# Thirty-two experts in 16 rounds instead of 18: fixed experts share their rounds with three of the smallest

## The reference, cut to what matters

```python
g_logits = (xt @ lp['rg_w'] + lp['rg_b']).astype(jnp.float32)
_, g_idx = lax.top_k(g_logits, 1)                       # 1 of 4 groups
...
top_v, top_i = lax.top_k(e_logits, TOP_K)               # 2 of its 8 experts
expert_idx = g_idx * EXPERTS_PER_GROUP + top_i
...
def run(args):
    xb, e = args
    return (jax.nn.silu(xb @ wg[e]) * (xb @ wu[e])) @ wd[e]
...
return jnp.einsum('nk,nkd->nd', w, ys[slot])
```

## Time and profile before

| | |
|---|---|
| three runs | 1404.47, 1409.8, 1411.97 us, median 1409.8 |
| profiled execution | 1408.7 us, its span 1406.9 us |
| PE, DVE, ACT, POOL busy | 87%, 51%, 20%, 8% of the span |
| mean DMA rate | 238 GB/s over the span |
| `up` (L2160), U and ring tiles | 174.9 + 132.4 us busy |
| `down` (L2193), U and ring tiles | 90.8 + 50.7 us busy |
| gathers (L580), scatters (L587) | 36 and 36 |

### The profile page before, as it was taken

The page is one execution under the profiler, slowest core; times in us unless marked ns, Lnnn a source line. Parts: engine busy times, 40 slices in busy tenths (PEclk is TensorE's granted clock), DMA queues, the critical chain, the costliest instruction groups (busy, mean ns, idle before and its releaser), DMA issues.

```text
span 1406.9 us, 19405 instructions
## 1 busy us (share of the span) xinstructions
PE 1218.9 (87%) x7082; PEld 710.5 (50%) x7082; DVE 722.8 (51%) x1639; ACT 284.4 (20%) x708; POOL 112.9 (8%) x171
## 2 busy tenths in 40 slices
PE   5999999889886798999959999988989579898891
PEld 3455545554452565566424554556445356566560
DVE  3365877782476132332362687877643723332334
ACT  1211153750121000000022103357211110000000
POOL 2000000001001111111000000000100011111100
PEclk9999999999888999999989999999999779999996
DMA  9321101347149999999960201014562399999996
GB/s 375 150 94 50 54 17 61 129 177 308 41 177 401 416 418 418 418 418 417 410 252 31 90 33 60 1 68 181 198 252 104 138 398 418 417 418 417 419 415 250
DMA packets 61199, 334.54 MB, mean 238 GB/s; under 512 B 11856, under 2 KB 11856, under 8 KB 29100
## 3 DMA queue, kind: packets, MB, share of 16 engines
q1 hardware_dynamic: 45504, 295.78, 52.2%
q0 software_dynamic: 15600, 37.50, 7.0%
HBM read 322.41 MB, written 27.61 MB: 249 GB/s over the span
## 4 chain that ended last, share of the span: by engine, by line
PE 50%; DMA 27%; DVE 10%; issue 4%; ACT 3%; DVEq 2%; SPq 1%; PEld 1%; POOL 1%; PEldq 0%; ACTq 0%; POOLq 0%
DMA U<-in_stream 14%; PE bank L1748 12%; PE bank L1679 9%; PE bank L2160 8%; DMA ring<-in_stream 8%; PE bank L2193 6%; PE bank L2047 4%; DMA U<-in_n2row 3%; PE bank L1623 1%; DVE U L1267 1%; PE bank L1836 1%; DMA U<-moe_out 1%; PE bank L1862 1%; PE bank L2141 1%; SPq L382 1%
## 5 line engine op out<-in xcount | busy, mean ns | idle before, releaser
L2160 PE MATMUL bank<-U,HT 128*64 128x256 f32 (+2 forms) x1088 | 174.9, 400 | 24.2 <-DMA U<-in_stream 16.5
L1748 PE MATMUL bank<-HT,ring 128*128 128x512 f32 (+1 forms) x640 | 175.4, 435 | 2.0 <-issue 2.0
L1679 PE MATMUL bank<-ring,HT 128*128 128x512 f32 x320 | 147.0, 601 | 2.9 <-ACT HT L649 1.5
L2160 PEld LDWEIGHTS bank<-U,HT 128*64 128x64 f32 (+2 forms) x1088 | 117.8, 147 | 62.4 <-issue 40.1
L2160 PE MATMUL bank<-ring,HT 128*64 128x256 f32 (+2 forms) x736 | 132.4, 402 | 12.8 <-DMA ring<-in_stream 9.1
L1748 PEld LDWEIGHTS bank<-HT,ring 128*128 128x128 f32 x640 | 97.3, 191 | 79.7 <-issue 79.7
L1110 DVE SCALAR_TENSOR_TENSOR U<-U,prm 128x655 f32<-128x655 f32 x120 | 107.9, 899 | 8.0 <-issue 0.8
L2160 PEld LDWEIGHTS bank<-ring,HT 128*64 128x64 f32 (+2 forms) x736 | 86.4, 154 | 46.2 <-issue 28.6
L2047 PE MATMUL bank<-ring,HT 128*128 128x512 f32 x240 | 106.6, 594 | 0.0
L1541 DVE TENSOR_TENSOR HT<-bank,HT 128x256 f32<-128x256 f32 x36 | 15.3, 424 | 174.4 <-ACT HT L879 174.4
L2193 PE MATMUL bank<-U,HT 128*64 128x512 f32 (+2 forms) x288 | 90.8, 596 | 9.5 <-DMA U<-in_stream 6.0
(11 more groups left out here) (363 smaller groups left out, 1652.2 us busy)
## 6 DMA issues: line engine op xcount, KB each, us to landing
ring<-in_stream SPq DMA_DIRECT2D x138, 1024.0 KB, 7.3
U<-in_stream SPq DMA_DIRECT2D x96, 1024.0 KB, 22.7
RAB<-in_stream SPq DMA_DIRECT2D x16, 1024.0 KB
U<-moe_out SPq DMA_DIRECT2D x20, 512.0 KB, 7.4
U<-in_stream SPq DMA_DIRECT2D x16, 512.0 KB
CAT<-in_stream SPq DMA_DIRECT2D x16, 512.0 KB
RAB<-mod_rows POOLq DMA_DIRECT2D x12, 512.0 KB, 8.8
moe_in<-CAT POOLq DMA_DIRECT2D x10, 512.0 KB, 3.3
```

The source lines that it names most:

```text
L1679: ins = e.matmul(bank[:], HT[:, k, t * P:(t + 1) * P], wide(q, k), start=(k == 0), stop=(k == KD - 1))
L1748: ins = e.matmul(out, wt(q)[:, k, P * (n % 2):P * (n % 2) + P], HT[:, k, lo:lo + w], start=(k == 0), stop=(k == KD - 1))
L2160: ins = e.matmul(PS[2 + p][s, FF * j:FF * j + FF], xgT[:, p, k, s], w, start=(k == 0), stop=(k == KD - 1))
```

## The change

The three rounds F keep their fixed expert, but give it 96 slots instead of 128: 64 in one half of the block and 32 in the next quarter. The last 32 slots take one of the three smallest experts. So 29 others remain to be placed: 4 in B, 14 in P, 8 in Q and 3 beside the fixed ones. That makes 16 rounds, in the order P P F P F Q B P F B P B Q B P P. The third fixed expert moves from round 11 to round 8.

`sides(r)` now returns for an F round three pieces, of which the first two use the same tile. In odd blocks the halves are swapped. `whole` says whether a piece is the last one that reads its tile; only there the place is released. The loader still loads the fixed experts' nine tiles first, and the small experts' tiles of F rounds in the order of use.

```diff
-FIXED, BIGS, MIDS, SMALLS = 3, 8, 16, 8
+FIXED, BIGS, MIDS, SMALLS = 3, 7, 14, 8
 NR = BIGS + MIDS // 2 + SMALLS // 4
+BESIDE = BIGS + MIDS + SMALLS
-ROUNDS = list("PPFPFQBPBPPFBQBBPP")
+ROUNDS = list("PPFPFQBPFBPBQBPP")
 def round_blocks():
-    blocks = {"F": [(n, (n,)) for n in range(FIXED)],
+    blocks = {"F": [(n, (n, BESIDE + n)) for n in range(FIXED)],
...
 def tiles_loaded():
-    return sorted(tiles_used(), key=lambda tile: ROUNDS[tile[0]] != "F")
+    blocks = round_blocks()
+    return sorted(tiles_used(), key=lambda tile: blocks[tile[0]][1][tile[2]] >= FIXED)
...
+                apart, beside = small(1280, NE), small(1320, NE)
                 e.tensor_scalar(capm, rank, float(BIGS), float(HALF), ALU.is_lt, ALU.mult)
                 e.tensor_scalar(step, rank, float(BIGS + MIDS), float(QUART), ALU.is_lt, ALU.mult)
                 e.scalar_tensor_tensor(out=at0, in0=rank, scalar=float(BIGS + MIDS), in1=rank, op0=ALU.min, op1=ALU.add)
-                e.tensor_scalar(small(1660, NE), rank, float(BIGS), 2.0, ALU.min, ALU.mult); dr()
+                e.tensor_scalar(small(1660, NE), rank, float(BIGS), 2.0, ALU.min, ALU.mult)
+                e.tensor_scalar(apart, rank, float(FIXED), float(-QUART), ALU.is_lt, ALU.mult)
+                e.tensor_scalar(beside, rank, 3.0, float(3 - 4 * BESIDE - 3 * BIGS - MIDS), ALU.mult, ALU.add); dr()
                 e.tensor_tensor(capm, capm, step, ALU.add)
-                e.tensor_tensor(at0, at0, small(1660, NE), ALU.add); dr()
+                e.tensor_tensor(at0, at0, small(1660, NE), ALU.add)
+                e.scalar_tensor_tensor(out=beside, in0=rank, scalar=float(BESIDE), in1=beside, op0=ALU.is_ge, op1=ALU.mult); dr()
+                e.tensor_tensor(capm, capm, apart, ALU.add)
+                e.tensor_tensor(at0, at0, beside, ALU.add); dr()
                 e.tensor_scalar(at0, at0, float(QUART), None, ALU.mult)
...
                 def sides(r):
-                    n = P // len(blocks[r][1])
-                    return [(a, slice(n * a, n * a + n)) for a in range(P // n)]
+                    n, lanes_of = blocks[r]
+                    if n < FIXED:
+                        q = 64 * (n % 2)
+                        return [(0, slice(q, q + 64), False), (0, slice(64 - q, 96 - q), True), (1, slice(96 - q, P - q), True)]
+                    w = P // len(lanes_of)
+                    return [(a, slice(w * a, w * a + w), True) for a in range(P // w)]
...
-                        for a, s in both:
+                        for a, s, whole in both:
                             key = (l, r, j, a)
                             w = half_tile(key, k // 4)[:, FF * (k % 4):FF * (k % 4) + FF]
                             ins = e.matmul(PS[2 + p][s, FF * j:FF * j + FF], xgT[:, p, k, s], w,
                                            start=(k == 0), stop=(k == KD - 1))
...
-                            if k == KD - 1:
-                                if j and (a, s) == both[-1]:
+                            if k == KD - 1 and whole:
+                                if j and s == both[-1][1]:
```

More of the change, by code:

```diff
@@ L69, in round_blocks @@
 def round_blocks():
-    blocks = {"F": [(n, (n,)) for n in range(FIXED)],
-              "B": [(n, (n,)) for n in range(FIXED, BIGS)],
-              "P": [(BIGS + n, tuple(BIGS + 2 * n + (a + n) % 2 for a in range(2))) for n in range(MIDS // 2)],
-              "Q": [(BIGS + MIDS // 2 + n, tuple(BIGS + MIDS + 4 * n + (a + 2 * n) % 4 for a in range(4))) for n in range(SMALLS // 4)]}
+    blocks = {"F": [(n, (n, BESIDE + n)) for n in range(FIXED)],
+              "B": [(n, (n,)) for n in range(FIXED, BIGS)]}
+    for kind, first, lane, w in (("P", BIGS, BIGS, 2), ("Q", BIGS + MIDS // 2, BIGS + MIDS, 4)):
+        count = (MIDS if w == 2 else SMALLS) // w
+        blocks[kind] = [(n, tuple(lane + w * (n - first) + (a + n % 2 * w // 2) % w for a in range(w)))
+                        for n in range(first, first + count)]
     return [blocks[kind].pop(0) for kind in ROUNDS]
@@ L2161, in up @@
                                            start=(k == 0), stop=(k == KD - 1))
-                            if k == 0 and (a, s) == both[-1]:
+                            if k == 0 and s == both[-1][1]:
                                 settle(ins)
-                            if k == KD - 1:
-                                if j and (a, s) == both[-1]:
+                            if k == KD - 1 and whole:
+                                if j and s == both[-1][1]:
                                     ins.then_inc(S["gu_ps"], 1)
@@ L2194, in down @@
                                                start=(k == 0), stop=(k == 1))
-                                if k == 0 and j == 0 and (a, s) == both[-1]:
+                                if k == 0 and j == 0 and s == both[-1][1]:
                                     settle(ins)
-                                if k and j:
-                                    if (a, s) == both[-1]:
+                                if k and j and whole:
+                                    if s == both[-1][1]:
                                         ins.then_inc(S["y2_ps"], 1)
```

## The result

| | median us | runs | ratio to before, with its interval |
|---|---|---|---|
| before | 1410.88 | 1404.47 to 1412.26 | |
| after | 1433.2 | 1423.97 to 1435.01 | 1.0154 [1.0113, 1.0195] |

The change makes the kernel slower by 22 us, 1.5%: the interval does not include 1, and the time is outside the range of the prediction (1404 to 1420). The profiled execution took 1435.0 us with a span of 1433.2 us, against 1408.7 and 1406.9.

A forecast was written before the change was run, and what follows sets the result against it. Transfers, full at 418 GB/s in the expert stages, bound the kernel. 1408.7 us profiled + 0.6 VectorE + 0.1 last scatter = 1409.4, or 1410.5 as median; own range 1406 to 1415, with the drained case's ends 1404 to 1420.

The forecast's parts named there:

- the paragraph on TensorE: TensorE, fixed rounds: three products of 64, 32, 32 columns cost 0 more than one; two rounds fewer give 24.8 us per layer.
- the widths do not run side by side: Rival, fixed rounds: width changes drain TensorE, 13.6 us per fixed round, 0 to 5 us per layer, about 1415; chance 0.18.
- bound of 22 us: Rival, fixed rounds: three pieces wholly one behind another, 22 us per round, 23 us per layer, about 1456; chance 0.06.
- the air: TensorE, one stage: 18.6 us of tile waits plus 24.8 from removed rounds, 43.4 us, covers 42 us of extra work.
- count of places: Loader, fixed rounds: places hold tiles ahead, six at first, nine from round 3, twelve from round 5; no gap, 0.
- Bytes: Transfers, expert stages: same tiles and used rows before and after, so the stretch keeps its length; term 0.
- VectorE: Before the table `lanes`: five more instructions, smaller block tables; 0.60 us, counted in layer 1, 0 in layer 0.
- The tiles come last: End of the expert stage: set by a tile, narrowly; last up product waits 0.38 us, last but one down 0.56.
- Two rounds fewer ... go into waits for tiles: TensorE, each layer: 24.8 us saved become waits for tiles, which grow from 18.6 to some 43 us.
- Pace by rounds: Rival, expert stages: the rounds set the pace, so two rounds of 12.4 us go per layer, 1361; chance 0.04.
- sign of its own failure: Fixed rounds: `up` over 5 us, DMA share under 1 in rounds 2 to 5, or plateaus ending earlier would show it wrong.

The follow-up runs named there:

- round 2: Changed kernel with 64, 32 and 32 columns only in round 2, four pieces of 32 in rounds 4 and 8: 1417.76 us, ratio 1.0069 to before.
- round 4: Changed kernel with 64, 32 and 32 columns only in round 4, four pieces of 32 in the other F rounds: 1410.82 us, ratio 1.0013 to before.
- rounds 2 and 4: Changed kernel with four pieces of 32 columns in round 8; the other two F rounds keep 64, 32 and 32: 1430.83 us, ratio 1.0148 to before.
- round 8: Changed kernel with 64, 32 and 32 columns only in the third F round, four pieces of 32 in the others: 1409.91 us, ratio 1.0020 to before.
- all, grouped: Changed kernel; in F rounds the 64-column piece runs through all its steps first, then the two of 32: 1413.74 us, ratio 1.0034 to before.
- before, rounds 2, 4, 11: Kernel before, 18 rounds, its three F rounds cut into 64, 32 and 32 columns of the same tile: 1470.78 us, ratio 1.0438 to before.
- the first experiment: Changed kernel with the 64-column piece cut into two of 32, so quarters in all F rounds: 1409.26 us, ratio 1.0000 to before.

## Why the prediction was wrong

**The step that failed** is in the paragraph on TensorE: "Widths mixed in one step are not in this trace ... I take 0, since both neighbours, two and four groups, are at it". The neighbours were at 0 because each has one width. The term is 15.2 us per fixed round. The rival "the widths do not run side by side" had the mechanism, from a place in the trace where widths meet, and nearly the size: a step of 1.06 us (measured 1.13), +4.8 per `up` (5.4), +4.0 in `down` (4.4), 13.6 in all. It had a chance of 0.18. Against it stood "that no two widths below 128 meet in the trace", and that was a misreading: at the end of round 3 of the kernel before, `down` with 64 columns runs right ahead of `gate` with 32.

```profile
1195.50 3.65 PE L2193 MATMUL bank<-U,HT 128*64 128x512 f32 x16
```

It ends at 1199.15, so its last instruction of 0.59 us starts at 1198.56; the first product of 32 columns starts at 1199.08, 0.52 us later and just before that end, where products of one width follow at 0.43. The seam between 64 and 32 was there to be read. The rule of the Trainium skill behind it (page "TensorEngine Tiling (Array Packing)", section Key Properties: a change of tiling mode drains TensorE) agrees with these runs, at 9.07 against 7.19 us for many switches against one. The prediction's bound of 22 us, at 0.06, had all three pieces in a row; it did not come, since the two of 32 columns still share their time.

**The second error** would have made even the rival too cheap (1415). "Even with 0 to 14 us per fixed round the total stays within the air" compares sums over a stage, and air at its end doesn't help a queue that stands still at its start. The rival's price of 0 to 5 us per layer does not follow from its own numbers either: 30 us behind, with the 23 us of the nine places that round 4 has, are 7 us per layer, about 1424.5 in all. The prediction's own count of places does it, once 15.2 is put in and the places are those of that round (worked out afterwards). A fixed round then takes PE 12.4 + 15.2 = 27.6 us against 9.1 of transfers, so PE falls back 18.5 us; a P round between regains 4.2. Six places in circulation at round 2 are 15.1 us, nine at round 4 are 22.6, twelve at round 8 are 30.1.

| mixed in | behind, less places | measured, layer 0 and 1 |
|---|---|---|
| round 2 | 18.5 - 15.1 = 3.4 | 3.9, 7.4 |
| round 4 | 18.5 - 22.6, none | -0.7, 2.9 |
| rounds 2 and 4 | 37.0 - 4.2 - 22.6 = 10.2 | 9.2, 10.4 |
| round 8 | 18.5 - 30.1, none | -0.5, 1.4 |
| all, grouped | 2 x 13.9 - 4.2 - 22.6 = 1.0 | 2.7, 1.8 |
| all (the change) | 10.2 | 8.7, 11.0 |
| before, rounds 2, 4, 11 | 2 x 26.0 - 4.2 - 22.6 = 25.2 | 32.8, 32.0 |

The table was made after the results, though the expectations of the four kernels with mixed widths in some rounds rest on the same idea and stood before they ran. Its misses are up to 4 us in a layer, and it doesn't say why layer 1 loses more with round 2 or 4 alone. The last line fits worst because the count holds only while the transfers end the stage. There TensorE did, and for layer 1 the sum over the stage gives 31.3 us.

**What was right.** Bytes: 37.50 MB before and after, and with quarters the plateau is as long as before, so the term of 0 holds. VectorE: 0.18 + 0.11 + 0.37 = 0.66 predicted for the three stages, 0.69 measured; with -0.06 for the tables 0.60 predicted, and 0.6 more wait of SP. The tiles come last in both kernels. "Two rounds fewer ... go into waits for tiles": shown by the first experiment, with 35.0 us where the prediction had some 43. The 24.8 us did not all become waits: PE's own work got 9.7 us longer than expected, 5.4 of them in rows at a lower granted clock behind waits. No kernel separates the clock from the waits. "Pace by rounds" (1361) is excluded by the same experiment. The prediction named the sign of its own failure: an `up` over 5 us and a DMA share under 1 in rounds 2 to 5.

**What stays open.** Of the 26.3 us between the two profiled spans, 19.7 are in the stages and 0.6 in each layer's table; some 5 are in code that is the same, where runs of one kernel differ by as much.

## What to carry to other kernels

A cost that no row shows is not the cost of its neighbours, when what is new is the mixture: where one row shows a seam between them, price the mixture from the seam. To use unequal shares of TensorE's columns side by side, cut them all to the smallest width (64 and 32 and 32 as four of 32); this cost nothing here, and where it can't be done, group the widths so that they switch once. Whether a slow stretch costs time in a kernel bound by transfers has two limits. One is the places free in that very stretch: compare how far the engine falls behind, round by round, with the bytes that can still be sent. The other is the air of the whole stage. The change failed the first, and the kernel before with mixed widths failed both.

## What the runs showed of the hardware that I had not expected

A float32 product of 32 columns beside one of 64, in other column groups, starts only 0.37 us behind the last instruction of 64, and the next one of 64 0.31 us behind the last of 32, where two of 32 columns start 0.01 us apart. So unlike widths don't share their time: each step with both takes 1.13 us instead of 0.46, while two of 64 or four of 32 share 3.67 for eight steps. Cutting one product of 128 columns into four of 32 of the same weights costs nothing (3.66 against 3.72 us), though it is 64 instructions and 64 weight loads instead of 16.

With less work on TensorE its granted clock was lower. Over 495 to 560 us PE with quarters is busy for 50.48 us at a mean of 0.92; before it was:

```profile
495.00:560.00 65.00, 58.63 (x432) 36.71 (x432) 21.18 (x30) 4.88 (x10) 10.10 (x10) 0.97 1.02 418
```

The time of the kernel didn't change, because the transfers set the pace there.
